# Down projection: weight sums formed one slab later, the products of a quad in another order, one quad in the last trip, fewer constant matmuls at the start

## The chip, the cores and the metric

One core of one Trainium2 chip. The metric is the device time of one execution in microseconds (us); given is the median of the runs. Engines: TensorE (PE; its weight loads are PEld), VectorE (DVE), ScalarE (ACT), GpSimd (POOL), SyncE (SP), which issues all DMAs.

## What is computed

One layer of a hybrid decoder trunk on x (1 x 256 x 2048, fp32), cut to what matters here:

```python
def reference(x, ...):                  # D_MODEL 2048, SEQ 256, D_FF 8192, DEPTH 1
    h = rmsnorm(x, norm_mix_g[l])
    u = h @ w_in[l]                      # 2048 x 12800: conv branch, short conv, q, k, v, gates
    ...
    x = x + merged @ w_mix_out[l]
    h = rmsnorm(x, norm_ffn_g[l])
    x = x + jnp.square(jax.nn.relu(h @ w_up[l])) @ w_down[l]
    return rmsnorm(x, final_g)
```

The change concerns the last product, with `w_down` (8192 x 2048), and the first microseconds.

## The kernel before, in words

Every weight goes through SBUF once, in slabs of 512 KB, as fp32. To keep fp32 accuracy each slab is split in two parts of type fp32r: ScalarE copies it to `w_hi` (L503), VectorE subtracts (`w_lo = w_raw - w_hi`, L729); activations are split likewise, and a product is three matmuls: high by high, high by low, low by high. I call the subtraction "the residual" of a slab.

**The ring.** `w_raw`, `w_hi` and `w_lo` have four slots. At step k of a trip TensorE works on slab k, and ScalarE and VectorE prepare slab k+3 (LOOKAHEAD 3). ScalarE may start that when slab k-1 is used (`slab_used`); SyncE loads slab s into its `w_raw` slot once the residual of slab s-4 is done (`lo_done`, L406 to L415).

**Stages.** After the input projection, three branches and the mixing projection, the feed-forward part runs in 4 chunks c of 2048 hidden channels. In each: 4 trips of the up projection (8 slabs, two groups of 4; at a group's end VectorE evacuates it, L1191 on), then 2 trips of the down projection of 16 slabs k = 0 to 15, each for 1024 output columns (n = 0, 1 by 512). The first and last chunk are written out, the middle two are a loop. Down products have tokens on the output partitions; a plain slab is 2 inner tiles x 2 token blocks x 3 = 12 matmuls of 512 columns (L1319 to L1321), accumulated in banks 4 to 7. VectorE adds banks to `y_tok` at the end of a trip (`corner_sums`, L790, and `token_sums`, L769 to L783).

**Quads.** The slabs (n=0, i) and (n=1, i) for odd i = 3, 5, 7 follow each other, at k = 6, 10, 14. There the work of both slabs is a 2 x 2 block product (two token blocks by two inner tiles, times two inner tiles by the two column halves n), done by seven products in place of eight (the Strassen-Winograd form): 21 matmuls in place of 24 (`products_quad`, L1326). Sums of activations (S1 to S4, in `a_forms`) are made during the up projection; sums of weights (T1 to T4, in `w_sums`) are made by VectorE per quad: T1 and T3 in one instruction from both raw slabs (`forms_first`, L740), T2 from T1 and T4 from T2 (`forms_second`, L747, L750). "Doubly summed" are T2 and T4, S2 and S4. They are split as the weights are: ScalarE makes `w_forms[0]` (L509, L511), VectorE `w_forms[1]` (`forms_lo`, L756), two sums at a time. `t_lo` counts these halves. P2, P3 and P4 go into the banks of the plain products; P1, P5, P6 and P7 into banks 0 to 3, which `token_sums` adds up. The last trip (c=3, t=1) has quads at k = 6 and 10 only, so that its end is plain.

Before, VectorE's program of a trip has `forms_first` of quad kq at step kq-4 and `forms_second` at kq-3, and the halves of `forms_lo` at kq-2 (T2, T4) and kq-1 (T1, T3). TensorE's order is P2, P4, P3, P1, P6, P7, P5. In the last trip VectorE also makes `gains` of the finished columns at step 4 (L818) and ScalarE their squares at step 3 (L525).

**The start.** TensorE transposes x (L1370) in parts as they land. Constant matmuls (ones by identity, results unused) stand before them (WARM, 6, L1382) and after the first four tiles (WARM_GAP, 20, L1400); each is two rows of the trace. Four more tiles follow, then the first product, which waits for `w_lo` of slab 0 (`prologue`, L822).

## Time and profile before

| | |
|---|---|
| median of 3 runs | 1520.77 us (1520.45 to 1520.98) |
| the profiled execution | 1521.96 us |
| its span | 1519.9 us |
| TensorE busy | 1505.6 us (99%) |
| VectorE busy | 1190.9 us (78%) |
| ScalarE busy | 756.1 us (50%) |
| DMA | 290.86 MB, mean 191 GB/s |
| granted TensorE clock, mean | 0.998 |

The span runs from the first to the last instruction of the profiled execution. Busy times of TensorE are sums of overlapping durations cut to the span; a pitch (start to start) says more. A timeline row gives start, duration, engine, line, operation and operands, and in brackets how long the engine was idle before it and what ended that.

### The profile page before, as it was taken

What the parts mean: (1) busy time and instruction counts of PE and PEld (TensorE: products, weight loads), DVE (VectorE), ACT (ScalarE), POOL (GpSimd) and SP (SyncE); (2) the same over time, 40 slices, a digit from 0 to 9 for tenths busy, and PEclk for the clock granted to TensorE, in tenths of its full rate; (3) what the DMA queues carried; (4) which work ended last, traced back from release to release, by engine and by line L of the source; (5) the groups of instructions that cost most, each with busy time, mean ns of one, the idle gap of its engine ahead of it and who ended that gap; (6) DMA issues with size and microseconds to landing.
All of it is one profiled execution on the core that took longest, in us unless ns stands there. A gap on an engine that the chain in (4) does not pass through costs nothing. (4 is left out here: it accounts for less than half of the span.)

```text
span 1519.9 us, 22403 instructions
## 1 busy us (share of the span) xinstructions
PE 1505.6 (99%) x7670; PEld 1270.0 (84%) x7670; DVE 1190.9 (78%) x1578; ACT 756.1 (50%) x942; POOL 2.0 (0%) x11
## 2 busy tenths in 40 slices
PE   9999999999999999999999999999999999999997
PEld 8888888877778888888888888888888888888885
DVE  6568888988889877565556779987798779887798
ACT  5544444465554455444445445545455545544553
POOL 0000000000000000000000000000000000000000
PEclk9999999999999999999999999999999999999999
DMA  7655566655556556656555655655656565566553
GB/s 240 194 180 190 187 195 199 196 182 173 171 171 193 194 194 211 194 195 199 181 180 171 197 186 208 207 190 170 207 190 211 170 211 199 181 196 203 204 198 138
DMA packets 209961, 290.86 MB, mean 191 GB/s; under 512 B 9227, under 2 KB 129107, under 8 KB 209778
## 3 DMA queue, kind: packets, MB, share of 16 engines
q1 hardware_dynamic: 209906, 290.14, 58.2%
q8 instruction: 33, 0.54, 0.2%
q14 instruction: 22, 0.18, 0.0%
HBM read 287.48 MB, written 2.10 MB: 191 GB/s over the span
## 5 line engine op out<-in xcount | busy, mean ns | idle before, releaser
L503 ACT ACTIVATE w_hi<-w_raw 128x1024 fp32r<-128x1024 f32 x510 | 532.8, 1056 | 458.0 <-PE acc L1321 266.2
L729 DVE TENSOR_TENSOR w_lo<-w_raw,w_hi 128x1024 fp32r<-128x1024 f32 x510 | 614.6, 1221 | 170.6 <-ACT w_hi L503 165.8
L1297 PE MATMUL acc<-h_hl,w_hi 128*128 128x512 f32 x1740 | 546.7, 395 | 0.0
L1295 PEld LDWEIGHTS acc<-h_hl,w_lo 128*128 128x128 f32 x1740 | 322.3, 188 | 72.7 <-issue 0.6
L1295 PE MATMUL acc<-h_hl,w_lo 128*128 128x256 f32 x1740 | 343.6, 279 | 0.0
L1297 PEld LDWEIGHTS acc<-h_hl,w_hi 128*128 128x128 f32 x1740 | 265.2, 189 | 0.0
L1319 PE MATMUL acc<-w_hi,m_hl 128*128 128x512 f32 x456 | 177.8, 390 | 0.0
L1321 PE MATMUL acc<-w_hi,m_hl 128*128 128x512 f32 x456 | 177.4, 389 | 0.0
L1320 PE MATMUL acc<-w_lo,m_hl 128*128 128x512 f32 x456 | 177.4, 389 | 0.0
L1319 PE MATMUL acc<-w_hi,h_hl 128*128 128x512 f32 x384 | 151.5, 394 | 0.0
L1321 PE MATMUL acc<-w_hi,h_hl 128*128 128x512 f32 x384 | 149.6, 389 | 0.0
L1320 PE MATMUL acc<-w_lo,h_hl 128*128 128x512 f32 x384 | 149.5, 389 | 0.0
L869 DVE SCALAR_TENSOR_TENSOR conv<-glu,par,conv (+1 forms) x240 | 108.8, 479 | 7.0 <-DVE conv L869 5.8
L1321 PEld LDWEIGHTS acc<-w_hi,m_hl 128*128 128x128 f32 x456 | 85.6, 188 | 17.8
L1320 PEld LDWEIGHTS acc<-w_lo,m_hl 128*128 128x128 f32 x456 | 85.6, 188 | 17.7
L1319 PEld LDWEIGHTS acc<-w_hi,m_hl 128*128 128x128 f32 x456 | 85.6, 188 | 17.6
L1319 PEld LDWEIGHTS acc<-w_hi,h_hl 128*128 128x128 f32 x384 | 72.1, 188 | 17.1 <-DVE w_lo L729 2.7
L661 ACT ACTIVATE second<-acc 128x512 f32<-128x512 f32 x58 | 34.7, 599 | 102.6 <-PE acc L1297 102.6
L1321 PEld LDWEIGHTS acc<-w_hi,h_hl 128*128 128x128 f32 x384 | 72.1, 188 | 15.2
L1320 PEld LDWEIGHTS acc<-w_lo,h_hl 128*128 128x128 f32 x384 | 72.1, 188 | 14.4
L1191 DVE TENSOR_TENSOR pair<-acc,second 128x512 f32<-128x512 f32 x54 | 37.3, 691 | 55.0 <-ACT second L661 54.9
L698 ACT ACTIVATE m_hl<-pair 128x512 f32 (+1 forms) x32 | 20.2, 632 | 74.1 <-DVE pair L1242 74.1
(202 smaller groups left out, 1472.8 us busy)
## 6 DMA issues: line engine op xcount, KB each, us to landing
w_raw<-in_w_in SPq DMA_DIRECT2D x200, 512.0 KB, 3.5
w_raw<-in_w_up SPq DMA_DIRECT2D x128, 512.0 KB, 4.3
w_raw<-in_w_down SPq DMA_DIRECT2D x128, 512.0 KB, 4.4
w_raw<-in_w_mix_out SPq DMA_DIRECT2D x32, 512.0 KB, 3.6
w_raw<-in_w_sconv_out SPq DMA_DIRECT2D x16, 512.0 KB, 4.2
w_raw<-in_w_attn_out SPq DMA_DIRECT2D x16, 512.0 KB, 3.9
w_raw<-in_w_conf_out SPq DMA_DIRECT2D x16, 512.0 KB, 4.2
bias_row<-in_gate_b SPq DMA_DIRECT2D x12, 256.0 KB, 3.9
```

The lines of the kernel that those rows point to most:

```text
L503: act.activation(w_hi[:, q], w_raw[:, q], ACT.Copy).then_inc(hi_done, 1)
L661: act.activation(second[:, :, :], acc[:, b:b + 2, SEQ:], ACT.Copy).then_inc(half_copied, 1)
L698: act.activation(m_hl[:, bass.ds(j * 2, 2), 0, :], pair[n][:, :, :], ACT.Copy).then_inc(hid_hi, 1)
L729: dve.tensor_tensor(w_lo[:, q], w_raw[:, q], w_hi[:, q].bitcast(F32), ALU.subtract).then_inc(lo_done, 1)
L869: dve.scalar_tensor_tensor(dst, src, w, dst, ALU.mult, ALU.add).then_inc(step, 1)
L1191: dve.tensor_tensor(dst, halves[0], second[:, :, :], ALU.add).then_inc(half_sum, 1)
L1295: pe.matmul(*narrow[m], start=False, stop=False)
L1297: last = pe.matmul(*wide[m], start=False, stop=final)
L1319: pe.matmul(acc[:, b + m, :], h_h, hi[:, a, :], start=first, stop=False)
L1320: pe.matmul(acc[:, b + m, :], h_h, lo[:, a, :], start=False, stop=False)
L1321: last = pe.matmul(acc[:, b + m, :], h_l, hi[:, a, :], start=False, stop=final)
```

## The change

1. WARM_GAP goes from 20 to 6.
2. VectorE makes T1 and T3 one step later (at kq-3, after the residual of slab kq) and T2 and T4 one step later (at kq-2). ScalarE and VectorE split T1 and T3 first, T2 and T4 second.
3. TensorE's products of a quad come in another order: P2, P1, P3, P7, P5, P6, P4, and in a closing quad (the last one of a trip, k=14, but not in the last trip) P2, P4, P3, P1, P7, P5, P6.
4. The last trip has one quad, k=10.
5. SyncE waits for one residual more (`late`) before it loads the slabs k = 10 and 14 of a down trip (those whose slot held the first slab of a quad) and k = 2 of every up and down trip.

```diff
--- before.py
+++ after.py
@@ -131,7 +131,7 @@
 
     if ph.name != "down":
         return ()
-    return (6, 10) if last_trip(ph, c, t) else (6, 10, 14)
+    return (10,) if last_trip(ph, c, t) else (6, 10, 14)
 
 
 def quad_of(ph, c, t, k):
@@ -157,7 +157,7 @@
 MIX_T = 2
 X_PARTS = ((0, 256), (256, 512), (512, 1024), (1024, 1536), (1536, 2048))
 WARM = 6
-WARM_GAP = 20
+WARM_GAP = 6
 
 
 def walk(eng, body):
@@ -406,8 +406,9 @@
 
 
                 shared = ph.name == "B"
+                late = k - RING in quads(ph, c, t) or ph.name in ("up", "down") and k == 2
                 if not (isinstance(s, int) and s < RING or shared and k == KDOWN):
-                    sp.wait_ge(lo_done, s + (shared and k == KDOWN - 1) - (RING - 1))
+                    sp.wait_ge(lo_done, s + (shared and k == KDOWN - 1) + late - (RING - 1))
                 if ph.name in TOKEN_ROWS:
                     sp.dma_start(wide_rows(w_raw[:, k % RING]), w[bass.ds(row, DROWS), bass.ds(col, DCOLS)]
                                  .rearrange("(a p) n -> p a n", p=P)).then_inc(raw_full[k % RING], 16)
@@ -505,10 +506,11 @@
             def forms_hi(ph, c, t, k):
 
                 if k + 2 in quads(ph, c, t):
-                    act.wait_ge(t_raw, quad_of(ph, c, t, k + 2) * 2 + 2)
+                    act.wait_ge(t_raw, quad_of(ph, c, t, k + 2) * 2 + 1)
+                    act.activation(w_forms[:, 0, 0:2, :], w_sums[:, 0:2, :], ACT.Copy).then_inc(t_hi, 1)
+                if k + 1 in quads(ph, c, t):
+                    act.wait_ge(t_raw, quad_of(ph, c, t, k + 1) * 2 + 2)
                     act.activation(w_forms[:, 0, 2:4, :], w_sums[:, 2:4, :], ACT.Copy).then_inc(t_hi, 1)
-                if k + 1 in quads(ph, c, t):
-                    act.activation(w_forms[:, 0, 0:2, :], w_sums[:, 0:2, :], ACT.Copy).then_inc(t_hi, 1)
 
             def first_product(ph, c, t, k):
 
@@ -752,7 +754,7 @@
 
             def forms_lo(ph, c, t, k, part):
                 dve.wait_ge(t_hi, quad_of(ph, c, t, k) * 2 + part + 1)
-                two = slice(2, 4) if part == 0 else slice(0, 2)
+                two = slice(0, 2) if part == 0 else slice(2, 4)
                 dve.tensor_tensor(w_forms[:, 1, two, :], w_sums[:, two, :], w_forms[:, 0, two, :].bitcast(F32),
                                   ALU.subtract).then_inc(t_lo, 1)
 
@@ -1067,13 +1069,13 @@
                         dve.reciprocal(mix_stat[:, 3, :], mix_stat[:, 2, :]).then_inc(inv1, 1)
                         dve.wait_ge(inv1, 1)
                         spread_diagonal(diag1)
-                    if k + 3 in quads(ph, c, t):
-                        forms_second(ph, c, t, k + 3)
+                    if k + 2 in quads(ph, c, t):
+                        forms_second(ph, c, t, k + 2)
                     if ph.name == "down" and k == 15 and not last_trip(ph, c, t):
                         corner_sums(c, t)
                     lo(ph, c, t, k)
-                    if k + 4 in quads(ph, c, t):
-                        forms_first(ph, c, t, k + 4)
+                    if k + 3 in quads(ph, c, t):
+                        forms_first(ph, c, t, k + 3)
                     if k + 2 in quads(ph, c, t):
                         forms_lo(ph, c, t, k + 2, 0)
                     if k + 1 in quads(ph, c, t):
@@ -1347,24 +1349,41 @@
                     pe.matmul(acc[:, at, :], rows[0], columns[1], start=False, stop=False)
                     return pe.matmul(acc[:, at, :], rows[1], columns[0], start=False, stop=stop)
 
+                def corner(name):
+                    if name == "P2":
+                        return product(4, whole(0, 2 * i + 1), loaded(w_x, 1), False, closing)
+                    if name == "P3":
+                        pe.wait_ge(lo_done, s + 2)
+                        pe.wait_ge(f_lo, c * 4 + i // 2 + 1)
+                        return product(6, form(S4), loaded(w_y, 1), False, closing)
+                    pe.wait_ge(t_lo, quad * 2 + 2)
+                    return product(5, whole(1, 2 * i + 1), summed(T4), False, closing)
+
+                def shared(name):
+                    if name == "P1":
+                        if first and not (isinstance(c, int) and c == 0 and isinstance(t, int) and t == 0):
+                            pe.wait_ge(p_sum, pair_of(c, t) * P_SUMS)
+                        return product(P_BANK[name], whole(0, 2 * i), loaded(w_x, 0), first, final)
+                    rows, f = {"P6": (S2, T2), "P7": (S3, T3), "P5": (S1, T1)}[name]
+                    pe.wait_ge(t_lo, quad * 2 + (2 if name == "P6" else 1))
+                    return product(P_BANK[name], form(rows), summed(f), first, final)
+
                 pe.wait_ge(lo_done, s + 1)
-                product(4, whole(0, 2 * i + 1), loaded(w_x, 1), False, closing)
-                pe.wait_ge(t_lo, quad * 2 + 1)
-                last = product(5, whole(1, 2 * i + 1), summed(T4), False, closing)
+                corner("P2")
                 if closing:
-                    last.then_inc(c_full, 1)
-                pe.wait_ge(lo_done, s + 2)
-                pe.wait_ge(f_lo, c * 4 + i // 2 + 1)
-                last = product(6, form(S4), loaded(w_y, 1), False, closing)
-                if closing:
-                    last.then_inc(c_full, 1)
-                if first and not (isinstance(c, int) and c == 0 and isinstance(t, int) and t == 0):
-                    pe.wait_ge(p_sum, pair_of(c, t) * P_SUMS)
-                product(P_BANK["P1"], whole(0, 2 * i), loaded(w_x, 0), first, final).then_inc(slab_used, 1)
-                product(P_BANK["P6"], form(S2), summed(T2), first, final)
-                pe.wait_ge(t_lo, quad * 2 + 2)
-                product(P_BANK["P7"], form(S3), summed(T3), first, final)
-                product(P_BANK["P5"], form(S1), summed(T1), first, final).then_inc(slab_used, 1)
+                    corner("P4").then_inc(c_full, 1)
+                    corner("P3").then_inc(c_full, 1)
+                    shared("P1").then_inc(slab_used, 1)
+                    shared("P7")
+                    shared("P5")
+                    shared("P6").then_inc(slab_used, 1)
+                else:
+                    shared("P1").then_inc(slab_used, 1)
+                    corner("P3")
+                    shared("P7")
+                    shared("P5")
+                    shared("P6")
+                    corner("P4").then_inc(slab_used, 1)
 
             def transposed(dst, src):
                 return pe.transpose(dst, src, ident[0:src.shape[0], 0:src.shape[0]])
```

What this does to VectorE's program, in a down trip from the residual of slab 5 on (k=6 is the first quad). Before:

```order
L729 TENSOR_TENSOR w_lo<-w_raw,w_hi 128x1024 [waits hi_done] x3
L740 TENSOR_TENSOR w_sums<-w_raw 128x1024 [waits raw_full3,raw_full2]
L747 TENSOR_TENSOR w_sums<-w_raw,w_sums 128x512 [waits t_raw]
L750 TENSOR_TENSOR w_sums<-w_raw,w_sums 128x512 [waits t_two]
L729 TENSOR_TENSOR w_lo<-w_raw,w_hi 128x1024 [waits hi_done]
L726 TENSOR_TENSOR w_lo<-w_raw,w_hi 128x512 [waits hi_done]
L756 TENSOR_TENSOR w_forms<-w_sums,w_forms 128x1024 [waits t_hi]
L729 TENSOR_TENSOR w_lo<-w_raw,w_hi 128x1024 [waits hi_done]
L756 TENSOR_TENSOR w_forms<-w_sums,w_forms 128x1024 [waits t_hi]
```

and now:

```order
L731 TENSOR_TENSOR w_lo<-w_raw,w_hi 128x1024 [waits hi_done] x4
L742 TENSOR_TENSOR w_sums<-w_raw 128x1024 [waits raw_full3,raw_full2]
L749 TENSOR_TENSOR w_sums<-w_raw,w_sums 128x512 [waits t_raw]
L752 TENSOR_TENSOR w_sums<-w_raw,w_sums 128x512 [waits t_two]
L728 TENSOR_TENSOR w_lo<-w_raw,w_hi 128x512 [waits hi_done]
L758 TENSOR_TENSOR w_forms<-w_sums,w_forms 128x1024 [waits t_hi]
L731 TENSOR_TENSOR w_lo<-w_raw,w_hi 128x1024 [waits hi_done]
L758 TENSOR_TENSOR w_forms<-w_sums,w_forms 128x1024 [waits t_hi]
```

A residual (L729 before, L731 now, x3 and x4: the fourth is slab 6's) has moved from behind the three sums to ahead of them; the two subtractions of `w_forms` stand where they were.

TensorE's program at the first quad of a trip; of each product the first of its three matmuls. Operands name it: `w_hi,m_hl` P2 and P1, `w_forms,m_hl` P4, `w_hi,a_forms` P3, `w_forms,a_forms` P5 to P7. Before:

```order
L1346 MATMUL acc<-w_hi,m_hl 128x512 [waits lo_done,hid_lo]
...
L1346 MATMUL acc<-w_forms,m_hl 128x512 [waits t_lo]
...
L1346 MATMUL acc<-w_hi,a_forms 128x512 [waits f_lo,lo_done]
...
L1346 MATMUL acc<-w_hi,m_hl 128x512
...
L1346 MATMUL acc<-w_forms,a_forms 128x512
...
L1346 MATMUL acc<-w_forms,a_forms 128x512 [waits t_lo]
...
L1346 MATMUL acc<-w_forms,a_forms 128x512
```

and now:

```order
L1348 MATMUL acc<-w_hi,m_hl 128x512 [waits lo_done,hid_lo]
...
L1348 MATMUL acc<-w_hi,m_hl 128x512
...
L1348 MATMUL acc<-w_hi,a_forms 128x512 [waits f_lo,lo_done]
...
L1348 MATMUL acc<-w_forms,a_forms 128x512 [waits t_lo]
...
L1348 MATMUL acc<-w_forms,a_forms 128x512 [waits t_lo]
...
L1348 MATMUL acc<-w_forms,a_forms 128x512 [waits t_lo]
...
L1348 MATMUL acc<-w_forms,m_hl 128x512 [waits t_lo]
```

The product P4, which was second and waited for a half of the forms, is last; the first wait for `t_lo` is now at the fourth product.

The same in the closing quad now:

```order
L1348 MATMUL acc<-w_hi,m_hl 128x512 [waits lo_done,hid_lo]
...
L1348 MATMUL acc<-w_forms,m_hl 128x512 [waits t_lo]
...
L1348 MATMUL acc<-w_hi,a_forms 128x512 [waits f_lo,lo_done]
...
L1348 MATMUL acc<-w_hi,m_hl 128x512
...
L1348 MATMUL acc<-w_forms,a_forms 128x512 [waits t_lo]
...
L1348 MATMUL acc<-w_forms,a_forms 128x512 [waits t_lo]
...
L1348 MATMUL acc<-w_forms,a_forms 128x512 [waits t_lo]
```

P4 is second as before; its wait for `t_lo` is for the second half (`quad * 2 + 2`), where it was for the first.

TensorE at the start, before and now:

```order
L1382 MATMUL acc<-ident,ones 128x128 x6
L1370 MATMUL acc<-ident,y_tok 128x128 x8
L1400 MATMUL acc<-ident,ones 128x128 x20
L1370 MATMUL acc<-ident,y_tok 128x128 x8
L1290 MATMUL acc<-h_hl,w_hi 128x512 x2
```

```order
L1401 MATMUL acc<-ident,ones 128x128 x6
L1389 MATMUL acc<-ident,y_tok 128x128 x8
L1419 MATMUL acc<-ident,ones 128x128 x6
L1389 MATMUL acc<-ident,y_tok 128x128 x8
L1292 MATMUL acc<-h_hl,w_hi 128x512 x2
```

Between the transposes of the first four tiles and those of the next, six constant matmuls stand in place of 20.

## Rows read from the trace of the kernel before

**Rows 1.** The page: busy time, share of the span, instructions

```profile
PE 1505.6 (99%) x7670; PEld 1270.0 (84%) x7670; DVE 1190.9 (78%) x1578; ACT 756.1 (50%) x942; POOL 2.0 (0%) x11
```

**Rows 2.** Timeline before and in a closing quad (k=14): TensorE, ScalarE, VectorE

```profile
1285.15 0.39 PE L1319 MATMUL acc<-w_hi,m_hl 128*128 128x512 f32 x1
...
1287.87 0.39 PE L1346 MATMUL acc<-w_hi,m_hl 128*128 128x512 f32 x1
...
1285.35 1.06 ACT L503 ACTIVATE w_hi<-w_raw 128x1024 fp32r<-128x1024 f32 x1
...
1286.91 1.22 DVE L729 TENSOR_TENSOR w_lo<-w_raw,w_hi 128x1024 fp32r<-128x1024 f32 x1
1288.05 1.22 DVE L756 TENSOR_TENSOR w_forms<-w_sums,w_forms 128x1024 fp32r<-128x1024 f32 x1
```

**Rows 3.** Waits of TensorE: line waited for, us in total, times, longest us

```profile
PE acc L1346 <- DVE w_forms L756: 2.1, 3, 1.6
```

**Rows 4.** Timeline, quad k=6 of the last trip: start us, us, engine, instruction [idle before]

```profile
1482.03 0.39 PE L1346 MATMUL acc<-w_hi,m_hl 128*128 128x512 f32 x1
...
1487.44 0.50 PE L1346 MATMUL acc<-w_forms,a_forms 128*128 128x512 f32 x1 [1.65 <-DVE w_forms L756]
...
1488.94 0.39 PE L1319 MATMUL acc<-w_hi,m_hl 128*128 128x512 f32 x1
...
1482.63 2.49 DVE L818 TENSOR_TENSOR yg_tok<-y_tok,gf_row 128x512 f32<-128x512 f32 x4
...
1486.18 1.22 DVE L756 TENSOR_TENSOR w_forms<-w_sums,w_forms 128x1024 fp32r<-128x1024 f32 x1
```

**Rows 5.** Timeline, first quad of a second trip, TensorE and VectorE

```profile
1309.41 0.39 PE L1348 MATMUL acc<-w_hi,m_hl 128*128 128x512 f32 x1
1310.07 0.50 PE L1346 MATMUL acc<-w_forms,m_hl 128*128 128x512 f32 x1 [0.27 <-DVE w_forms L756]
1310.40 0.40 PE L1347 MATMUL acc<-w_forms,m_hl 128*128 128x512 f32 x1
...
1304.47 1.23 DVE L740 TENSOR_TENSOR w_sums<-w_raw 128x1024 f32<-128x1024 f32 x1 [2.10 <-DMA w_raw<-in_w_down]
...
1308.80 1.22 DVE L756 TENSOR_TENSOR w_forms<-w_sums,w_forms 128x1024 fp32r<-128x1024 f32 x1
```

**Rows 6.** Timeline, end of an up trip; last, landings of loads issued 1285.5, 1286.2 us

```profile
1223.91 0.37 SPq L415 DMA_DIRECT2D w_raw<-in_w_up  x1
...
1226.22 1.06 ACT L503 ACTIVATE w_hi<-w_raw 128x1024 fp32r<-128x1024 f32 x1 [1.73 <-PE acc L1297]
...
1227.31 1.23 DVE L729 TENSOR_TENSOR w_lo<-w_raw,w_hi 128x1024 fp32r<-128x1024 f32 x1 [1.30 <-ACT w_hi L503]
1229.75 0.69 DVE L1191 TENSOR_TENSOR pair<-acc,second 128x512 f32<-128x512 f32 x1 [1.21 <-ACT second L661]
...
1234.83 3.50 DVE L729 TENSOR_TENSOR w_lo<-w_raw,w_hi 128x1024 fp32r<-128x1024 f32 x3
...
1237.19 0.39 PE L1295 MATMUL acc<-h_hl,w_lo 128*128 128x256 f32 x2
...
DMA to landing us min/median/max: 4.0/4.7/5.4
```

**Rows 7.** Timeline of the start; last, landing of the load issued at 2.7 us

```profile
2.61 2.93 PE L1382 MATMUL acc<-ident,ones 128*128 128x128 f32 x12
...
7.04 4.66 PE L1400 MATMUL acc<-ident,ones 128*128 128x128 f32 x40
11.53 1.04 PE L1370 MATMUL acc<-ident,y_tok 128*128 128x128 f32 x8
12.32 0.70 PE L1290 MATMUL acc<-h_hl,w_hi 128*128 128x512 f32 x2
...
9.09 1.23 DVE L822 TENSOR_TENSOR w_lo<-w_raw,w_hi 128x1024 fp32r<-128x1024 f32 x1
...
DMA to landing us min/median/max: 6.3/6.3/6.3
```

## The prediction

> **What bounds the kernel now.** I read the page first. TensorE is busy for 99% of the span [rows 1], so the time is the number of its matmuls times their pitch, plus the few places where it stands still, plus its start and its end. The pitch is read from a slab of the down projection: twelve 512-column matmuls start between 1285.15 and 1287.87 us, 2.72 us, or 0.227 us each [rows 2]. The 389 ns that a row gives as a matmul's duration overlap; only starts are compared here.
>
> Then the waits of TensorE: it waited for VectorE's weight forms at three places [rows 3]. The timeline there has the details. In the first quad of the last trip (k=6) 21 matmuls would take 4.76 us; they take 1488.94 - 1482.03 = 6.91 us, so 2.15 us are lost, nearly all while VectorE does four gains (L818, 2.49 us) ahead of the form that P7 needs [rows 4]. In the first quad of a second trip 1310.07 - 1309.41 = 0.66 us stand where 0.23 would, and the next start is 0.33 after instead of 0.23: 0.43 + 0.10 = 0.53 us lost. In that trip VectorE's first sum had idled 2.10 us for a DMA [rows 5]. The third of the three waits is the same place one chunk earlier: of 2.1 us in total 1.65 and 0.27 are the two shown, which leaves 0.2 [rows 3], so about 0.50 us lost. The other 20 quads wait for nothing.
>
> From all these stalls comes one constant that I need below: TensorE starts 1310.07 - 1308.80 = 1.27 us, and 1487.44 - 1486.18 = 1.26 us, after the start of the VectorE subtraction (L756) that it waits for [rows 4, 5].
>
> **The change part by part.**
>
> *Last trip with one quad.* The quad of k=6 becomes two plain slabs, 24 matmuls in place of 21: + 3 x 0.227 = + 0.68 us. Its stall goes: - 2.15 us. VectorE loses that quad's sums and forms and has its gains (2.49 us) beside plain slabs, which need only 1.14 us of it per 2.72 us. The quad of k=10 had no stall before and has less work ahead of it now. Together - 1.47 us.
>
> *Sums begin a slab later.* The first sum (L740) came after the residual of slab kq-1 and waited for the landing of slab kq+1; it now comes after the residual of slab kq, which runs under that landing. For the trip of [rows 5]: the DMA lands as before, by 1304.47 us, but a residual that used to follow the sums is then already done. VectorE's later work moves up by that residual, 1.14 us from start to start [rows 2]: the first forms start near 1307.7 instead of 1308.80 and are needed, as the fourth product now, at 1308.95 + 9 x 0.227 = 1310.99; they are there at 1307.7 + 1.27. Both second-trip stalls go: - 0.53 - 0.50 = - 1.03 us.
>
> *Product order in the other quads (k=6 and 10, and the last trip's).* P4, which needs the forms of T2 and T4, is last, P6 one but last. Neither waits. The slab_used of the first slab comes after 6 matmuls instead of 12, 1.36 us sooner, so ScalarE and VectorE can run ahead. I count 0: TensorE is the bound there. Without this cover it would cost what a late form costs, 1.27 us after its start less the time left.
>
> *Product order in the closing quad (k=14, 7 of them).* This is the place that speaks against the change. P4 stays second, since its bank must be full for the corner sums; but it now waits for the second half of the forms, where it waited for the first. What orders them: ScalarE's w_hi of slab 16 starts 1285.35 - 1285.15 = 0.20 us after the slab before the last one ends on TensorE [rows 2]. VectorE's residual of it starts 1.09 us after it: the up projection shows 1226.22 to 1227.31 [rows 6]. The second form follows the residual by 1288.05 - 1286.91 = 1.14 us [rows 2], and TensorE by 1.27 us. Sum: 0.20 + 1.09 + 1.14 + 1.27 = 3.70 us from the beginning of the slab ahead of the quad. P4 is due after that slab and P2: 2.72 + 0.68 = 3.40 us. So 0.30 us of stall, and 0.10 us at the next start as in the stall of [rows 5]: 0.40 us, seven times, + 2.80 us. Today P7 is the one that waits for the second half, 2.7 us later in the quad, so nothing is seen. Bounds: 0 each if the hand-overs overlap more than I think (VectorE may start before its row says), and 0.8 each if it is as late as in [rows 2], where the second form started at 1288.05, 0.18 us after the quad began: 1288.05 + 1.27 - 1288.55 = 0.77. I take 0.40, since with the DMA wait gone VectorE is idle ahead of that residual.
>
> *Later loads.* Slabs k=10 and 14, and k=2 of every up and down trip, are now loaded one residual later, together with the next slab. In steady stretches a load lands well ahead of w_hi. The tight place is the end of an up trip. There the load of k=2 goes out with that of k=3, at 1223.91 us, instead of one residual earlier. Of two loads that go out 0.7 us apart in the down projection the first landed after 4.0 us, the second after 5.4 [rows 6]. That gives 1227.9 to 1228.1. w_hi then starts 1.8 us later than its 1226.22, the residual at 1229.1, and the evacuation of the group (L1191) at about 1230.3 instead of 1229.75. All that follows it moves by 0.5 us, the residual of k=3 to 1235.35; TensorE can take it 1.27 us later, at 1236.6, and needs it at 1237.19 [rows 6]. 0.6 us are left. Cost 0; from where it costs is in the rivals.
>
> *Fewer constant matmuls.* The 20 of the gap (40 rows, 4.49 us, 0.112 each) end at 11.53 us. Six end at 7.04 + 12 x 0.112 = 8.4 us. The transposes then wait for the third part of x, issued at 2.7 us and landed 6.3 us later, at 9.0 us [rows 7]; they take the 0.8 us of today (11.53 to 12.32), to 9.9. The first product waits for w_lo of slab 0, whose subtraction starts at 9.09 us whatever TensorE does: 9.09 + 1.27 = 10.36 instead of 12.32. - 1.96 us. The residuals of the next slabs follow the transposes and move along; their loads are out already. If one of them landed late, a part of the gain would go, which the lower bound covers. Bounds: 0 and 2.3.
>
> TensorE's clock is at stake here. The first constants (12 from 2.61 us, (2.93 - 0.43) / 11) start 0.23 us apart, the 40 later ones (4.49 / 40) 0.112 [rows 7]: the two levels, 1.2 and 2.4 GHz. The change opens two idle stretches, 0.6 and 0.4 us, with transposes between. The Trainium skill ("TensorE: Matmul & The Clock Gate", Part 4: PE-mode transpose) says that transposes do not count as activity in the way that matmuls do. By that rule the clock could fall again; by the rows, the clock had risen by 7.04 us although transposes filled the stretch just before. I take no fall, and price one below.
>
> **The sum.** - 1.47 - 1.03 + 2.80 + 0 - 1.96 = - 1.66 us. The profiled execution took 1521.96 us (its span is 1519.9, 2.1 lie around it) and would take 1520.3; the median of the runs, 1520.77, is 1.19 below it and goes to 1519.1 us. A measurement of this kernel tells 0.2%, 3.0 us, from no change; this is 0.1%.
>
> **The rivals.**
>
> *The closing quads don't stall* (the hand-overs are shorter, or VectorE's queue is ahead): - 1.66 - 2.80 = - 4.46 us, 1516.3. For it: today no closing quad loses anything. Against it: each of the four links has its row, and none depends on how early VectorE is, because the first is released by TensorE itself. Half a stall each gives 1517.7, the edge of 0.2%. Chance 0.24.
>
> *Late loads stall the up projection* (the other side: slower). Mechanism: the load of k=2 lands so late that the evacuation, and with it the residual of k=3, misses TensorE. It decides from 4.6 us of landing on (0.5 later than I took, since 0.6 us are left and the residual itself starts to push). The second loads of pairs do take 4.7 to 5.4 us; if the first took 5.1, 0.5 us are lost in each of 16 up trips, 8 us: 1527. For it: two loads are together on one queue and a third follows 1.2 us later. Against it: the first of a pair took 3.8 to 4.1 us in the down projection. Chance 0.10.
>
> *The clock falls in the start.* Half of any stretch at 1.2 GHz is lost. The first constants ran at that level, and by 7.04 us the engine was at the other, 4.4 us after it began [rows 7]; as long a stretch again costs 2.2 us, and the time is 1519.1 + 2.2 = 1521.3, still no change. Chance 0.12. That is what the page's rule would give.
>
> That a part does nothing at all can't be: each moves instructions on an engine that the rows show waiting or waited for.
>
> **How the numbers follow.** My forecast, 1519.1 us, has 0.54. Its own range is 1517.5 to 1520.5. Faster by over 0.2%: the first rival and a little of the forecast's lower end, 0.27. Slower by over 0.2%: the late loads, 0.10. Within: 0.63. The range from 1516.2 takes in the first rival and, up to 1522.0, the fall of the clock; the late loads are left out.
>
> **What would show it.** Right: the first 512-column product starts near 10.4 us; no stall at k=6 in second trips and in the last trip; TensorE's waits for w_forms all at k=14, seven of about 0.3 us; in the up projection no idle TensorE, and w_hi of k=2 waiting for its DMA once a trip. Wrong: gaps ahead of slab k=3 in up trips, a pitch of 0.45 us anywhere after 10 us, or closing quads of 4.76 us.

## The result, and the profile after

The changed kernel takes 1524.76 us (median of 19 runs, 1523.05 to 1527.00) where the kernel before, run beside it, takes 1521.93 (19 runs, 1520.31 to 1525.87): a ratio of 1.0018, 95% interval 1.0011 to 1.0025. It is slower, by 2.8 us. That is inside the 0.2% that the forecast called no change, but on the other side of zero, and outside the range of 1516.2 to 1522.0 us. (The kernel before ran 1.2 us slower here than in the three runs that the forecast started from; added to 1521.93 the forecast would be 1520.3, and the miss 4.5 us.) In all comparisons below one execution of one kernel, 2520.73 us at a granted clock of 0.556, is left out as disturbed. The span of the profiled execution is 1522.6 us, against 1519.9.

First the page, busy times (the answer to [rows 1]), then the waits of TensorE: line, line waited for, us in total, times, longest (the answer to [rows 3]).

```profile
PE 1504.9 (99%) x7645; PEld 1267.7 (83%) x7645; DVE 1187.6 (78%) x1573; ACT 756.5 (50%) x940; POOL 2.0 (0%) x11
```

```profile
PE acc L1348 <- DVE w_forms L758: 4.2, 6, 1.2
...
PE acc L1292 <- DVE w_lo L824: 0.5, 1, 0.5
PE acc L1297 <- DVE w_lo L731: 0.4, 1, 0.4
```

TensorE has 25 matmuls fewer (28 constants out, 3 in for the last trip's quad), as written. Its waits for forms are twice those of before, 4.2 us instead of 2.1, and there is a new one in the up projection (L1297). The first quad of a second trip, the place of [rows 5], now runs through; its fourth product starts 9 pitches after the quad, with the first half of the forms there in time. TensorE and VectorE of the changed kernel (start us, us, engine, instruction, [idle before]):

```profile
1311.21 0.39 PE L1348 MATMUL acc<-w_hi,m_hl 128*128 128x512 f32 x1
...
1313.25 0.39 PE L1348 MATMUL acc<-w_forms,a_forms 128*128 128x512 f32 x1
...
1315.97 0.39 PE L1321 MATMUL acc<-w_hi,m_hl 128*128 128x512 f32 x1
```

4.76 us for the quad: no stall. The last trip has none either ([rows 4] showed 2.15 us lost). The loss is in the closing quads. The longest of the seven, TensorE, ScalarE and VectorE in the timeline of the changed kernel (the answer to [rows 2]):

```profile
1456.62 1.06 ACT L504 ACTIVATE w_hi<-w_raw 128x1024 fp32r<-128x1024 f32 x1 [1.94 <-DMA w_raw<-in_w_down]
1457.72 1.23 DVE L731 TENSOR_TENSOR w_lo<-w_raw,w_hi 128x1024 fp32r<-128x1024 f32 x1 [0.66 <-ACT w_hi L504]
1458.86 1.22 DVE L742 TENSOR_TENSOR w_sums<-w_raw 128x1024 f32<-128x1024 f32 x1
...
1461.10 1.06 ACT L504 ACTIVATE w_hi<-w_raw 128x1024 fp32r<-128x1024 f32 x1
...
1462.05 1.22 DVE L758 TENSOR_TENSOR w_forms<-w_sums,w_forms 128x1024 fp32r<-128x1024 f32 x1
1463.18 1.22 DVE L731 TENSOR_TENSOR w_lo<-w_raw,w_hi 128x1024 fp32r<-128x1024 f32 x1
1463.56 0.39 PE L1348 MATMUL acc<-w_hi,m_hl 128*128 128x512 f32 x1
...
1464.32 1.22 DVE L758 TENSOR_TENSOR w_forms<-w_sums,w_forms 128x1024 fp32r<-128x1024 f32 x1
1465.59 0.50 PE L1348 MATMUL acc<-w_forms,m_hl 128*128 128x512 f32 x1 [1.19 <-DVE w_forms L758]
```

Read it upward from the stall. The second form (L758, 1464.32) releases TensorE 1.27 us later, as expected. The residual of slab 16 before it began at 1463.18, though its w_hi had started at 1461.10: it was due at 1462.19 and is 0.99 us late, because VectorE was not free. From 1457.72 on VectorE works back to back, residual of slab 14, three sums, residual, form, residual, form, 6.60 us from the first start to the last (three rows left out); and the residual at its head follows a w_hi (1456.62) that waited 1.94 us for its load. So the end of the chain is fixed by that landing, not by TensorE.

The load itself was not slow. In all seven trips the load of slab 14 landed 4.1 to 4.2 us after its issue; it was issued late. VectorE in this trip, and the two loads that went out at 1452.55 and 1452.96 us (slabs 14 and 15):

```profile
1446.75 2.58 DVE L731 TENSOR_TENSOR w_lo<-w_raw,w_hi 128x1024 fp32r<-128x1024 f32 x2 [1.49 <-ACT w_hi L504]
...
1451.83 0.69 DVE L728 TENSOR_TENSOR w_lo<-w_raw,w_hi 128x512 fp32r<-128x512 f32 x1
```

```profile
L413 SPq DMA_DIRECT2D w_raw<-in_w_down x2: 368/419/470, 1452.5 to 1453.0; - x2
...
DMA to landing us min/median/max: 4.1/4.6/5.2
```

The second residual of the first row is that of slab 10, done at 1449.33; L728 is the residual of slab 11 (half as long as the others, 128x512), done at 1452.52. Between the two now stand the three sums of the quad k=10. So "one residual later" means 3.19 us later, in this trip and in five of the other six (3.30 in one); in the kernel before the two residuals end 0.60 us apart.

In the fourth closing quad the same chain was early enough:

```profile
1149.36 1.06 ACT L504 ACTIVATE w_hi<-w_raw 128x1024 fp32r<-128x1024 f32 x1 [0.68 <-DMA w_raw<-in_w_down]
...
1155.11 1.06 ACT L504 ACTIVATE w_hi<-w_raw 128x1024 fp32r<-128x1024 f32 x1 [1.14 <-PE acc L1323]
...
1156.20 1.23 DVE L731 TENSOR_TENSOR w_lo<-w_raw,w_hi 128x1024 fp32r<-128x1024 f32 x1 [0.19 <-ACT w_hi L504]
...
1157.34 1.22 DVE L758 TENSOR_TENSOR w_forms<-w_sums,w_forms 128x1024 fp32r<-128x1024 f32 x1
...
1158.08 0.39 PE L1350 MATMUL acc<-w_hi,m_hl 128*128 128x512 f32 x1
...
1158.61 0.50 PE L1348 MATMUL acc<-w_forms,m_hl 128*128 128x512 f32 x1
1158.95 0.39 PE L1349 MATMUL acc<-w_forms,m_hl 128*128 128x512 f32 x1
```

Here VectorE stands idle ahead of the residual, each link is the one that the prediction priced (1.09, 1.14, 1.27), and TensorE loses 0.53 - 0.23 = 0.30 and 0.34 - 0.23 = 0.11 us. All seven closing quads of this profile, from their timelines (a quad without a stall takes 4.76 us):

| quad starts | w_hi of slab 14, before the quad | second form, after the quad's start | length |
|---|---|---|---|
| 941.65 | 8.09 | 0.01 | 5.51 |
| 983.89 | 8.58 | -0.23 | 5.27 |
| 1115.20 | 7.47 | 0.22 | 5.71 |
| 1157.63 | 8.27 | -0.29 | 5.21 |
| 1288.88 | 7.20 | 0.50 | 6.01 |
| 1331.61 | 7.32 | 0.38 | 5.91 |
| 1463.56 | 6.94 | 0.76 | 6.25 |

The lengths come to 6.55 us over 4.76 each; the two late starts of each quad, less a pitch, make up 6.27 of that, and I go on with this sum. In six of the seven w_hi of slab 14 waited for its load; in the second it was released by TensorE. What differs between the quads is how long before them that load went out, 11.0 to 13.1 us, hence how early VectorE was done with slabs 10 and 11. Where w_hi of slab 14 starts under 7.5 us before the quad, the form follows it by 7.7 us each time; where it starts earlier, the floor of -0.23 to -0.29 holds. In the first row the first sum waited for the landing of slab 15 besides.

The other place is one trip of the up projection, at 868 us. SyncE's load issues (durations in ns) and their landing:

```profile
L416 SPq DMA_DIRECT2D w_raw<-in_w_up x4: 372/372/1172, 854.6 to 856.9; - x4
...
DMA to landing us min/median/max: 5.4/6.7/7.3
```

and what followed, with the answer to [rows 6]. The load of k=2 is the first of the four; it landed after 5.4 us:

```profile
860.07 1.06 ACT L504 ACTIVATE w_hi<-w_raw 128x1024 fp32r<-128x1024 f32 x1 [4.82 <-DMA w_raw<-in_w_up]
...
867.24 2.36 DVE L731 TENSOR_TENSOR w_lo<-w_raw,w_hi 128x1024 fp32r<-128x1024 f32 x2
867.47 0.63 PE L1299 MATMUL acc<-h_hl,w_hi 128*128 128x512 f32 x2
868.52 0.50 PE L1297 MATMUL acc<-h_hl,w_lo 128*128 128x256 f32 x2 [0.43 <-DVE w_lo L731]
```

TensorE starts again 1.28 us after the residual. 868.52 - 867.47 = 1.05 us stand where two matmuls of this pitch take 0.46: 0.60 us lost, and 0.11 at the next start.

Last the start, the answer to [rows 7]:

```profile
7.18 1.85 PE L1419 MATMUL acc<-ident,ones 128*128 128x128 f32 x12
...
8.98 1.10 PE L1389 MATMUL acc<-ident,y_tok 128*128 128x128 f32 x8
...
9.25 1.23 DVE L824 TENSOR_TENSOR w_lo<-w_raw,w_hi 128x1024 fp32r<-128x1024 f32 x1
...
10.62 0.70 PE L1292 MATMUL acc<-h_hl,w_hi 128*128 128x512 f32 x2 [0.55 <-DVE w_lo L824]
```

The first product starts 1.70 us sooner (10.62, not 12.32), and the pitch after it is the fast one.

The account of the two profiles: start - 1.70; old stalls gone - 3.13; three matmuls more in the last trip + 0.68; closing quads + 6.27; up projection + 0.70. That is + 2.8 us, and the spans differ by 2.6 (1519.93 and 1522.55).

### The profile page after: what moved, and what is told of

Read it like the earlier page. It is cut to its first block and busy times, and to the rows that moved or that the text cites. A ratio compares the mean times of both kernels' runs of the same rounds, so it can differ in the third digit from the quotient of the medians.

```text
span 1522.6 us, 22350 instructions
## 1 busy us (share of the span) xinstructions
PE 1504.9 (99%) x7645; PEld 1267.7 (83%) x7645; DVE 1187.6 (78%) x1573; ACT 756.5 (50%) x940; POOL 2.0 (0%) x11
## 5 line engine op out<-in xcount | busy, mean ns | idle before, releaser
L731 DVE TENSOR_TENSOR w_lo<-w_raw,w_hi 128x1024 fp32r<-128x1024 f32 x511 | 615.6, 1222 | 216.8 <-ACT w_hi L504 212.0
L1297 PEld LDWEIGHTS acc<-h_hl,w_lo 128*128 128x128 f32 x1740 | 322.3, 188 | 73.2 <-DVE w_lo L731 0.9
L1297 PE MATMUL acc<-h_hl,w_lo 128*128 128x256 f32 x1740 | 343.7, 279 | 0.4 <-DVE w_lo L731 0.4
L1321 PE MATMUL acc<-w_hi,m_hl 128*128 128x512 f32 x464 | 180.9, 390 | 0.0
L1323 PE MATMUL acc<-w_hi,m_hl 128*128 128x512 f32 x464 | 180.6, 389 | 0.0
L1322 PE MATMUL acc<-w_lo,m_hl 128*128 128x512 f32 x464 | 180.5, 389 | 0.0
```

The source lines that it names most:

```text
L731: dve.tensor_tensor(w_lo[:, q], w_raw[:, q], w_hi[:, q].bitcast(F32), ALU.subtract).then_inc(lo_done, 1)
L1297: pe.matmul(*narrow[m], start=False, stop=False)
L1321: pe.matmul(acc[:, b + m, :], h_h, hi[:, a, :], start=first, stop=False)
L1322: pe.matmul(acc[:, b + m, :], h_h, lo[:, a, :], start=False, stop=False)
L1323: last = pe.matmul(acc[:, b + m, :], h_l, hi[:, a, :], start=False, stop=final)
```

## The experiments

Two theories. **The late loads:** a closing quad has a floor of 0.4 us, given by the forms alone; what lies above it comes from the loads of slabs k=10 and 14, now sent one residual later, whose landing VectorE's chain waits for. **The chain by itself:** the new order of sums and forms on VectorE makes the closing quads late whatever the loads do. Each kernel below was profiled once, and in five of them (the two single parts, P4 later, k=2 late only where it must be, the order alone) the profiled execution is the slowest counted: its rows show where the time goes, the medians how much. "Stalls" means matmul starts in the quads that come more than a pitch apart, summed.

### One part of the change alone: six constants, and one quad in the last trip

```diff
-WARM_GAP = 20
+WARM_GAP = 6
```

> The kernel before with WARM_GAP 6 and nothing else. In the changed kernel the first product started at 10.62 us instead of 12.32. Theory (the gain of the start is kept): the first product at 10.6, every later place 1.7 us sooner, the three stalls at k=6 as before, span 1518.2 us, time 0.11% less. Rival (it is given back): the first product is early, but loads that no longer keep up stop TensorE in the first 60 us, span near 1519.9.

Measured: 1521.86 us (11 runs) beside 1523.01, ratio 0.9991 (0.9982 to 1.0000). The first product starts at 10.98 us, 1.34 us sooner than in [rows 7], after 0.6 us of waiting for w_lo; 10.6 was expected. In this profile the old stalls came to 5.7 us instead of 3.1:

```profile
PE acc L1346 <- DVE w_forms L756: 3.5, 5, 1.7
```

The gain of the start stays in the time. A second lesson: the stalls of the kernel before are no constant, since they follow the landing of loads.

```diff
-    return (6, 10) if last_trip(ph, c, t) else (6, 10, 14)
+    return (10,) if last_trip(ph, c, t) else (6, 10, 14)
```

> The kernel before with quads (10,) in the last trip and nothing else. Theory (my term): three matmuls more, + 0.68 us, and the 2.15 us of the quad at k=6 of the last trip gone: span 1519.9 - 1.47 = 1518.4 us, 0.10% less. Rival: VectorE's gains and ScalarE's squares delay the quad k=10 instead, whose 4.76 us grow by up to 1 us: span 1519.4.

Measured: 1521.61 us beside 1523.01, ratio 0.9991 (0.9982 to 1.0000). The stall of the last trip is gone; 2.6 us are left in the others.

```profile
PE acc L1346 <- DVE w_forms L756: 1.0, 2, 0.6
```

The two parts give 1.15 and 1.40 us by the medians; if parts add up, the rest of the change costs some 5.4 us (2.83 + 1.15 + 1.40), an estimate across two comparisons.

### The loads late and not late, with the sums taken from a fixed tile

Sums that read w_raw are what makes the late load necessary, so the two can't be parted in the kernel as it is. Both kernels here take their sums from k_dup, a tile that stays, so their quads multiply other numbers and only their timing counts; the control keeps the late loads, the other sends them at the old time.

```diff
-                left = w_raw[:, x:x + 2, 0:2, :].rearrange("p s k b -> p s (k b)")
+                left = k_dup[:, :, :].rearrange("p (s k) b -> p s (k b)", s=2)
...
-                late = k - RING in quads(ph, c, t) or ph.name in ("up", "down") and k == 2
+                late = 0
```

(the last two lines in the second kernel alone)

> The changed kernel, with the sums of weights computed from a tile that no DMA writes (k_dup) instead of from w_raw: the seven products of a quad then multiply other numbers. Loads, waits, instruction counts and sizes stay. It is the control for the next run. Both theories: as the changed kernel, closing quads of 5.2 to 6.25 us (in sum 6.3 us over 4.76 each), one gap of 0.7 us in the up projection, span 1522.6 us.

> As e3_fixed_late, and the loads of k=10, 14 and 2 wait for one residual less, as before the change; nothing reads the raw slots late any more, so it is free of races. Theory (late loads): w_hi of slab 14 no longer waits for its DMA and starts 8.6 us before the closing quad in all seven, the second form 0.25 us before it; each closing quad takes 5.2 us, 3.2 us in sum over 4.76 instead of 6.3, and the gap in the up projection goes: span 1522.6 - 3.1 - 0.7 = 1518.8 us. Rival (VectorE's work, one slab later, is too much by itself, wherever the loads are): closing quads stay at 5.2 to 6.25 us, only the gap of 0.7 us goes: span 1521.9 us.

Measured: the control 1527.17 us, the other 1520.79 (one run each). Waits of TensorE in the control, then in the kernel without late loads:

```profile
PE acc L1348 <- DVE w_forms L758: 6.1, 7, 2.0
```

```profile
PE acc L1348 <- DVE w_forms L758: 0.6, 3, 0.2
```

Stalls of 8.4 us (0.5 of them in a quad k=10) and of 3.1 us in sum. The control was expected to repeat the changed kernel's span of 1522.6 and came to 1525.0; its stalls are larger, as in a later repetition of the changed kernel. Without late loads all seven closing quads lose the same, 0.31 to 0.37 us and 0.11 at the next start, and the gap in the up projection is gone. The last closing quad of that kernel, to be laid beside the one above:

```profile
1452.02 1.06 ACT L504 ACTIVATE w_hi<-w_raw 128x1024 fp32r<-128x1024 f32 x1 [0.30 <-PE acc L1350]
...
1459.24 1.22 DVE L731 TENSOR_TENSOR w_lo<-w_raw,w_hi 128x1024 fp32r<-128x1024 f32 x1 [0.18 <-ACT w_hi L504]
1460.38 1.22 DVE L758 TENSOR_TENSOR w_forms<-w_sums,w_forms 128x1024 fp32r<-128x1024 f32 x1
...
1461.65 0.50 PE L1348 MATMUL acc<-w_forms,m_hl 128*128 128x512 f32 x1 [0.21 <-DVE w_forms L758]
```

w_hi of slab 14 is released by TensorE, not by a load, 8.58 us ahead of the quad; its load had gone out at 1445.89, right behind the residual of slab 10, 14.7 us ahead of the quad where the control's went out 10.4 ahead. VectorE has the same instructions in the same order in both, so the chain by itself is ruled out as the cause of what lies above the floor; it takes the chain and the late load together. The span was expected at 1518.8 and is 1518.6.

### The product P4 later in the closing quad

```diff
-                    corner("P4").then_inc(c_full, 1)
-                    corner("P3").then_inc(c_full, 1)
+                    corner("P3")
                     shared("P1").then_inc(slab_used, 1)
                     shared("P7")
+                    corner("P4").then_inc(c_full, 2)
```

> The changed kernel with the closing quad in the order P2, P3, P1, P7, P4, P5, P6 (P4 fifth instead of second; the corner sums then start after it). Loads stay late. Theory (what costs is that P4 is due 0.68 us into the quad; the second form starts at most 0.8 us into it, so TensorE can have it at 2.1 us, and P4 is now due at 2.72): all closing quads take 4.76 us, span 1522.6 - 6.3 = 1516.3 us, 0.2% less than before. Rival (the corner sums, about 1 us later, push VectorE's token sums and then the next trip's forms): closing quads 4.76 us, but stalls at k=6 of second trips come back, span 1517.5 us or more.

Measured: 1522.40 us (10 runs, 1522.06 to 1523.39) beside 1523.16, ratio 0.9994 (0.9985 to 1.0004); span 1521.2. No closing quad waits for a form any more, but what stood behind P4 does: the corner sums (L792) start when VectorE has idled 1.02 us for them, and the next slab's first product waits. TensorE and VectorE at the end of the first closing quad:

```profile
945.98 2.35 DVE L792 TENSOR_TENSOR y_tok<-acc,y_tok 128x1024 f32<-128x1024 f32 x2 [1.02 <-PE acc L1350]
...
946.92 0.39 PE L1350 MATMUL acc<-w_forms,a_forms 128*128 128x512 f32 x1
947.36 0.47 PE L1321 MATMUL acc<-w_hi,m_hl 128*128 128x512 f32 x1
```

0.21 us there (0.44 less a pitch), and gaps of about the same size a few slabs into the next trips. Of the 6.3 us of closing stalls only 1.4 show in the span of this profile, but its first product also came 0.4 us later (11.00), its gap in the up projection took 1.0 us, and it is the slowest of the ten. By the medians, each against the kernel before run beside it, the edit gave 3.6 us (from + 2.8 to - 0.8): more than half of the closing stalls is regained, the rest moved to the next consumer. Of the rival the number came (a span over 1517.5) and the delay of the sums, but no stall at k=6 in second trips; the gaps stand around the trips' ends.

### The load of k=2 late only where it must be

```diff
-                late = k - RING in quads(ph, c, t) or ph.name in ("up", "down") and k == 2
+                late = k - RING in quads(ph, c, t) or after_quad and k == 2
```

after_quad holds for a trip that follows a closing quad and for no other (for this SyncE's loops have their first trips written out).

> The changed kernel, with the load of k=2 one residual later only in the trips that follow a closing quad (the others read no slab late there). k=10 and 14 stay late. Theory (each late load delays the copy of its slab, and the delay is handed on from quad to quad): the gap of 0.7 us in the up projection goes, and closing quads of first trips, 5.5 to 6.25 us, come down to 5.2 to 5.5: span near 1520.0 us. Rival (only the loads of k=10 and 14 matter in the down projection): only the 0.7 us go, span 1521.9.

Measured: 1524.07 us beside 1523.16, ratio 1.0005 (0.9996 to 1.0015). The gap in the up projection is gone; since it can also stay away by itself (see the last experiment), it takes the runs together to tie it to the load of k=2. The closing quads lost more than before in this profile, 9.2 us:

```profile
PE acc L1386 <- DVE w_forms L796: 7.3, 7, 1.6
```

so they don't need the late k=2 in that trip: the theory missed, and the span is 1524.7. Both edits together:

> Both edits, of e5_p4_later and e6_k2_needed. Theory: no stall in closing quads and no gap in the up projection, span 1522.6 - 6.3 - 0.7 = 1515.6 us, 0.28% less than before. Rival: as e5_p4_later, the up gap not being tied to k=2.

Measured: 1521.86 us beside 1523.16, ratio 0.9991 (0.9982 to 1.0000), span 1519.4; no wait of TensorE for forms and none in the up projection, gaps of 0.2 to 0.3 us at ten places around the trips' ends. Expected was 1515.6: both gaps went as foreseen, the price around the trips' ends was not foreseen.

### The loads of k=2 late, the others not

The fixed tile again, with only the loads of k=2 late.

```diff
-                late = k - RING in quads(ph, c, t) or ph.name in ("up", "down") and k == 2
+                late = ph.name in ("up", "down") and k == 2
```

> As e4_fixed_no_late (sums of weights from a fixed tile, so the quads multiply other numbers), with only the load of k=2 of up and down trips late again; k=10 and 14 load early. Theory (the closing quads wait because of the late loads of k=10 and 14, the gap in the up projection is the load of k=2): closing quads 5.2 us each as in e4, and the gap of 0.7 us at 868 us is back: span 1518.6 + 0.7 = 1519.3 us. Rival (the late load of k=2 starts the delay that is handed on): closing quads of first trips grow by 0.2 us or more, span over 1519.8.

Measured: 1522.38 us (one run), span 1520.1.

```profile
PE acc L1348 <- DVE w_forms L758: 1.4, 3, 1.0
```

Six closing quads stand at the floor (0.31 to 0.37), the last one lost 1.15 us; 3.9 us in sum instead of 8.4. The gap in the up projection is back, at 868 us, with 0.4 us instead of 0.7: the load of k=2 took 5.1 us. So the loads of k=10 and 14 make the closing stalls, and those of k=2 the other one.

The last quad left the floor for another late landing. In that trip `gf_row` is loaded too (L449, at 1433.68), and the loads of slabs 8 to 10 beside it took 6.7 to 9.7 us; w_hi waited 1.82 us for slab 8 and 2.04 for slab 9, and from 1446.38 on VectorE worked back to back until the late form at 1461.85. The kernel without late loads had landings of 6.2 to 8.9 us at the same place, and its chain caught up in time.

### Old sums with the new rest

The kernel before with six constants, the last trip's one quad, and P4 in fourth place (behind P3's) in quads that don't close; sums, forms and loads as before.

```diff
+                if closing:
+                    pe.wait_ge(t_lo, quad * 2 + 1)
+                    product(5, whole(1, 2 * i + 1), summed(T4), False, closing).then_inc(c_full, 1)
+                else:
...
+                    product(P_BANK["P1"], whole(0, 2 * i), loaded(w_x, 0), first, final).then_inc(slab_used, 1)
...
+                else:
+                    pe.wait_ge(t_lo, quad * 2 + 1)
+                    product(5, whole(1, 2 * i + 1), summed(T4), False, closing)
```

> The kernel before with WARM_GAP 6, one quad (k=10) in the last trip, and in quads that do not close P4 moved from second to fourth (P2, P1, P3, P4, P6, P7, P5); sums of weights, halves and loads stay as before, the closing quad too. Theory: the three gains add up, - 1.7 at the start, - 1.47 in the last trip, and the stalls at k=6 of second trips go, since the first form is due 1.36 us later and was 0.4 us late: - 1.0; span 1519.9 - 4.2 = 1515.7 us, 0.27% less than before. Rival: the stalls move to the closing quads, whose first form is still due after one product, span 1517.

Measured: 1519.64 us (11 runs, 1519.06 to 1520.47) beside 1523.16, ratio 0.9977 (0.9968 to 0.9986); span 1517.0. It beats both kernels.

```profile
PE acc L1346 <- DVE w_forms L756: 0.3, 1, 0.3
```

Stalls are down to 1.0 us. Against [rows 7] the start gained 1.5 us (first product at 10.79); the last trip has no stall, and the second trips little. The span is 1.3 us over the theory; it is the rival's number, but the stalls left stand at k=6 of second trips, not in the closing quads. Against the changed kernel, each beside the kernel before, this one is some 6.3 us faster: that is what the new sums and forms, with their order of products and the late loads, cost.

### The order of the products alone

> The kernel before with nothing but P4 fourth in the quads that do not close (P2, P1, P3, P4, P6, P7, P5). Theory: its first form is due 1.36 us later, which covers the stalls at k=6 and 10 of all trips but the last one, where the four gains stand ahead of the second half: stalls at w_forms fall from 3.1 us (5.7 in e1_gap6) to about 2: span 1518.8. Rival: slab_used comes earlier, but the stalls only move to the second half: span 1519.9.

Measured: 1525.27 us (10 runs) beside 1522.95, ratio 1.0012 (1.0002 to 1.0022): a miss, I had expected 1518.8. The forms in the last trip's first quad, which the kernel before has and the one just above has not, ended a wait of 2.27 us, and TensorE's clock fell at its end. Timeline, then stretches (us, PE busy, PEld, DVE, ACT, POOL, PEclk, DMA share, GB/s):

```profile
1490.31 0.79 PE L1346 MATMUL acc<-w_forms,a_forms 128*128 128x512 f32 x1 [2.27 <-DVE w_forms L756]
```

```profile
1488.00:1490.00 2.00, 0.04 (x1) 0.00 (x0) 2.00 (x2) 1.06 (x1) 0.00 (x0) 1.00 0.23 87
1490.00:1493.00 3.00, 2.69 (x6) 2.15 (x7) 2.97 (x4) 0.00 (x0) 0.00 (x0) 0.51 0.61 202
```

That quad took 8.56 us instead of 4.76. The first product came at 13.14 us besides, 0.8 later than in [rows 7]. The order did not make these forms later than they can be without it: the second form began 4.56 us after the quad's start, and in the kernel with six constants alone 4.74. There TensorE waited in two pieces, 0.65 us at P4 and 1.82 at P7; here P4 no longer waits, 2.43 us stand ahead of P7 in one piece, and the clock fell. In all three kernels (this one, the one before, the one with six constants) VectorE needs 9.01 us without a pause from the trip's first sum to this form, and that sum had idled 1.71, 1.43 and 1.91 us for a load: the landing sets where the form stands, the order only how the wait is cut up. Of the ten runs four lie at 1523.0 to 1523.9 us and six at 1525.2 to 1526.5, as if the fall came in some and not in others; with one profile, the slowest, that is not shown.

### No constants in the gap

```diff
-WARM_GAP = 20
+WARM_GAP = 0
```

> The kernel before with no constant matmul in the gap: TensorE idles from 7.1 us until the third part of x has landed at 9.0. Theory (the clock stays): the first product at 10.4 to 10.9 us as with six, matmuls after it 0.227 us apart. Rival (idle and transposes alone let the clock fall): matmuls after the first product are 0.45 us apart for a stretch, the kernel 1 to 2 us longer than with six.

Measured: 1524.63 us (one run), span 1522.5. TensorE's timeline and stretches (columns as above):

```profile
9.87 1.94 PE L1370 MATMUL acc<-ident,y_tok 128*128 128x128 f32 x8 [2.91 <-DMA y_tok<-in_x]
...
11.46 1.20 PE L1290 MATMUL acc<-h_hl,w_hi 128*128 128x512 f32 x2
```

```profile
9.00:12.00 3.00, 2.13 (x9) 2.07 (x10) 1.46 (x3) 1.05 (x4) 0.00 (x0) 0.66 1.04 359
12.00:14.00 2.00, 2.00 (x10) 1.77 (x9) 1.93 (x5) 1.63 (x3) 0.00 (x0) 0.66 1.07 392
```

After 2.91 us of idle the transposes and the first products run at a granted clock of 0.66 on average: for most of the stretch at the lower of the two levels, 1.2 GHz (the two products take 1.20 us where the changed kernel's row has 0.70). A hundred matmuls on, this kernel is 1.4 us behind the one with six constants (29.10 us against 27.73), 0.5 of it there already at the first product. The third rival of the prediction is real, with no constants in the gap; with six it did not come.

### The changed kernel once more

> The changed kernel once more, for the spread of its stalls on one chip. Theory (their size is set by when the late loads land): seven closing quads again, no two profiles with the same sizes, each as long as w_hi of slab 14 is late: sum 6 to 9 us over 4.76 each, none under 0.4 us. Rival (the order of the work sets it): the same seven sizes as before, 0.71, 0.48, 0.92, 0.42, 1.20, 1.09, 1.46 us within 0.1.

Measured: 1527.39 us (one run), span 1525.2; closing stalls 9.6 us in sum instead of 6.3, two quads at the floor again. The longest began like the one above, with w_hi of slab 14 6.27 us before the quad, waited 1.85 us and lost the clock as well:

```profile
1292.50:1294.00 1.50, 1.50 (x5) 1.14 (x4) 1.45 (x2) 0.00 (x0) 0.00 (x0) 0.59 0.99 358
1294.00:1297.00 3.00, 3.00 (x10) 2.37 (x9) 2.03 (x3) 1.54 (x2) 0.00 (x0) 0.63 0.76 248
```

That quad took 8.53 us, 1.6 of them by the clock (eight starts, 0.2 us further apart each), so the waits alone come to 8.0. The up projection had no gap this time; its load of k=2 landed after 4.2 us. Sizes thus change from run to run, which rules out the rival. In the four quads above the floor, the first one apart, the form follows w_hi of slab 14 by 7.7 us again. But the load of slab 14 landed 3.7 to 4.3 us after its issue in all seven; what changed is when VectorE let it go, 10.7 to 12.8 us ahead of the quad.

## Why the prediction was wrong, point by point

*Last trip with one quad*, - 1.47: right. Its stall is gone, and by itself the edit gave 1.4 us in the median. *Second-trip stalls*, - 1.03: right, they are gone. That the size fits so well is owed to reading it from the very profile compared with: in three other profiles with the old sums and the old order the same places lost 1.3, 1.8 and 2.1 us. *Fewer constants*, - 1.96: nearly. TensorE gained 1.70, because w_lo of slab 0 began at 9.25 instead of 9.09 and the product followed it by 1.37 us instead of 1.27. The six constants were not all at the fast pitch either (12 rows in 1.85 us, not 1.34), which that wait covered. The clock stayed up: in the changed kernel the first matmuls after the transposes are at the fast pitch. The Trainium skill ("TensorE: Matmul & The Clock Gate", Part 4: PE-mode transpose) says that transposes don't count as activity as matmuls do; with six constants and idle stretches of under 1 us around the transposes that rule cost nothing, nor with the 1.64 us of idle ahead of them in the run with P4 later (granted clock 1.00 to 14 us); without constants one cannot tell it from the 2.91 us of idle time.

*Closing quads*, + 2.80: this term failed. It was found at + 6.27, and 9.6 when repeated (1.6 of it by the clock). The chain of four links was right to 0.1 us wherever it bound: 0.42 to 0.48 us a quad, 3.1 us in all without late loads. The step that failed is the sentence "I take 0.40, since with the DMA wait gone VectorE is idle ahead of that residual". The DMA wait was not gone; it had moved one instruction back, from the sum to w_hi of slab 14. The prediction itself had said, a paragraph later, that slabs k=10 and 14 are loaded one residual later, and then priced only the load of k=2 ("In steady stretches a load lands well ahead of w_hi"). The landing was as its rows said (4.0 us for the first of a pair [rows 6], 4.1 here). What it never priced is the issue: the wait is for one residual more, and by the change itself three sums now stand ahead of that residual, so the load goes out 3.19 us later, not 0.6. In the quad at 1463.56 it was issued at 1452.5, w_hi could start at 1456.62, and VectorE's 6.6 us of work behind its residual then ended past the time of need. The upper bound of 0.8 a quad was too low as well, since it stopped at the position of the form in the kernel before, as if nothing could move it further out: three of the first profile's seven quads were inside it (0.45 to 0.75), four beyond (0.95 to 1.49).

*Product order in the other quads*, 0: held. All fifteen of them take 4.76 us in the changed kernel. On the old sums the order alone cost 2.3 us by the medians, which this term had no place for.

*Later loads*, 0: wrong in size, and the rival's mechanism right. It put the limit at 4.6 us of landing for the load of k=2 and the loss at 0.5 us for 5.1. Measured: up to 4.3 us lost nothing, 5.1 us 0.4, 5.4 us 0.7, 5.7 us 1.0 (the repetition, the run with k=2 alone late, the changed kernel, P4 later). But at most one trip in each profile got there; in the eleven others of the changed kernel in which w_hi waited for that load it landed after 3.8 to 4.0 us: + 0.70 us, not 8. The sign of the result comes from the closing quads.

The differences close the account: + 3.47 in closing quads, + 0.70 in the up projection, + 0.26 at the start, + 0.05 in old stalls, 4.5 us in sum. The forecast was - 1.66; measured + 2.83, 4.5 us apart. The rival of the falling clock (with six constants) did not come.

## What to carry to other kernels

When a change delays a load by even one instruction, look first at what stands between the old and the new instruction in that engine's program (here three sums, 3.19 us where it had been 0.60), then follow that load's consumer through the whole queue of the engine that uses it: a chain that runs back to back has no slack anywhere, and it passes a late landing on to its far end, here 7.7 us later. A product that waits earlier is only safe if the form it needs is early for its own reasons; bound a stall from issue plus landing, not from where the instruction stands today. Moving the wait to another consumer (P4 later) moved a good part of the loss with it; taking away what needed the wait (the old sums kept, a quad fewer, the constants out) gave 0.23%.

## What the runs showed of the hardware

A long stall can cost twice. After 2.27 us, 1.85 us and 2.91 us of idle TensorE the granted clock fell to 0.51 to 0.66 over the next stretches, and in the two quads among them six to eight matmuls came 0.43 us apart instead of 0.23, up to 1.6 us more. But 1.96 us of idle in the control with late loads, the 1.65 us of [rows 4] and 1.64 us at the start with P4 later were followed by a clock of 1.00, so the length of the idle time alone does not tell. I had thought of this danger only for the start.

In each closing quad that waited for a form, TensorE lost 0.11 us more at the second start after the wait (0.34 us where 0.23 would stand). Four loads that SyncE issued within 2.3 us took 5.4 to 7.3 us to land, and one of their issues 1172 ns instead of 372; a single one at 1448 us landed after 3.5. Beside the load of `gf_row` three loads took 6.7 to 9.7 us.
